# Products of constants on TensorE in the waits around the trunk norms of a two-layer diffusion backbone

## The reference

```python
def rms_norm(x, g):
    xf = x.astype(jnp.float32)
    y = xf * lax.rsqrt(jnp.mean(xf * xf, axis=-1, keepdims=True) + EPS)
    return (y * g.astype(jnp.float32)).astype(x.dtype)

def ffn_sublayer(t, shift, scale, gate, g_pre, g_post, w_in, w_out):
    y = swiglu(modulate(rms_norm(t, g_pre), shift, scale), w_in, w_out)
    return t + FFN_RES * gate * rms_norm(y, g_post)
```

## Time and profile before

| | us |
|---|---|
| median of three runs (lowest, highest) | 3044.97 (3043.56, 3045.20) |
| the profiled execution | 3045.96 |
| its span, first to last instruction | 3044.3 |

### The profile page before, as it was taken

One profiled execution on the slowest core, in us unless ns is written; L12 is line 12 of the kernel. 1 busy time (PEld: TensorE's weight loads), 2 busy tenths in 40 slices (PEclk: granted clock), 3 DMA queues, 4 the chain that ended last, 5 costly groups with the idle time before them and its releaser, 6 DMA issues.

```text
span 3044.3 us, 40240 instructions
## 1 busy us (share of the span) xinstructions
PE 2828.4 (93%) x14410; PEld 2251.5 (74%) x14410; DVE 1623.1 (53%) x2704; ACT 1209.9 (40%) x2223; POOL 220.4 (7%) x291
## 2 busy tenths in 40 slices
PE   6999989997799999997999979999889989999997
PEld 4888857875566676785888848888679667869897
DVE  4677236535544443345566246773365565545764
ACT  3222233235544434434222242222343555555543
POOL 0000011100000000001000010010111000001101
PEclk8999998999899999998999989999989989999899
DMA  5455323320011122132454315553233111324554
GB/s 230 166 193 186 98 96 136 106 90 28 28 42 36 42 77 73 35 118 86 144 172 167 94 54 193 193 191 95 76 108 125 70 56 63 108 84 152 196 174 134
DMA packets 94957, 343.70 MB, mean 113 GB/s; under 512 B 10994, under 2 KB 12786, under 8 KB 92658
## 3 DMA queue, kind: packets, MB, share of 16 engines
q1 hardware_dynamic: 74850, 263.45, 25.5%
q0 software_dynamic: 19984, 78.65, 7.3%
HBM read 337.85 MB, written 4.20 MB: 112 GB/s over the span
## 4 chain that ended last, share of the span: by engine, by line
PE 49%; DVE 4%; issue 4%; ACT 3%; POOL 1%; POOLq 0%; DVEq 0%; ACTq 0%
PE ps L1715 13%; PE ps L1723 13%; PE ps L1716 13%; PE ps L832 2%; PE ps L794 1%; PE ps L811 1%; PE ps L784 1%; DVE work L1526 1%; ACT work L1217 1%; PE ps L1773 1%; PE ps L1770 1%; PE ps L1775 1%; PE ps L790 1%; DVE mx L683 1%; POOL acc L934 1%
## 5 line engine op out<-in xcount | busy, mean ns | idle before, releaser
L1325 DVE TENSOR_TENSOR wlo<-raw,whi 128x1024 fp32r<-128x1024 f32 x492 | 597.4, 1223 | 658.5 <-ACT whi L1071 658.4
L1715 PE MATMUL ps<-xhi,whi 128*128 128x512 f32 (+1 forms) x2304 | 822.7, 368 | 53.7 <-DVE xlo L1559 44.7
L1716 PE MATMUL ps<-xlo,whi 128*128 128x512 f32 (+1 forms) x2304 | 810.3, 363 | 0.0
L1071 ACT ACTIVATE whi<-raw 128x1024 fp32r<-128x1024 f32 x492 | 520.6, 1058 | 565.2 <-PE ps L1723 494.6
L1715 PEld LDWEIGHTS ps<-xhi,whi 128*128 128x128 f32 x2304 | 443.3, 192 | 145.0 <-issue 45.9
L1723 PE MATMUL ps<-xhi,wlo 128*128 128x512 f32 (+1 forms) x2304 | 506.9, 363 | 0.0
L1716 PEld LDWEIGHTS ps<-xlo,whi 128*128 128x128 f32 x2304 | 445.1, 193 | 61.7
L1723 PEld LDWEIGHTS ps<-xhi,wlo 128*128 128x128 f32 x2304 | 396.0, 192 | 63.7 <-issue 0.7
L1473 DVE SCALAR_TENSOR_TENSOR work<-ada,work 128x1024 f32<-128x1024 f32 x256 | 299.3, 1220 | 0.3 <-DMA ada<-in_ada_rows 0.3
L1715 PE MATMUL ps<-ghi,whi 128*128 128x512 f32 (+1 forms) x704 | 252.2, 367 | 1.9 <-ACT whi L1071 1.9
L1716 PE MATMUL ps<-glo,whi 128*128 128x512 f32 (+1 forms) x704 | 251.8, 367 | 0.0
(11 more groups left out here) (199 smaller groups left out, 3373.8 us busy)
## 6 DMA issues: line engine op xcount, KB each, us to landing
raw<-in_ffn_in SPq DMA_DIRECT2D x176, 512.0 KB, 4.7
ada<-in_ada_rows POOLq DMA_DIRECT2D x128, 512.0 KB, 3.8
raw<-in_merge SPq DMA_DIRECT2D x96, 512.0 KB, 3.5
raw<-in_ffn_out SPq DMA_DIRECT2D x64, 512.0 KB, 3.5
raw<-in_qk_a SPq DMA_DIRECT2D x32, 512.0 KB, 3.5
raw<-in_ffn_out SPq DMA_DIRECT2D x32, 384.0 KB, 3.0
raw<-in_qk_b SPq DMA_DIRECT2D x20, 512.0 KB, 3.5
raw<-in_v_a SPq DMA_DIRECT2D x16, 512.0 KB, 3.5
```

What stands on the lines that cost most here:

```text
L1071: act.activation(whi[:, g.ring(SPLIT), :], raw[:, g.ring(RAW), :], ACT.Copy).then_inc(hi_ready, 1)
L1325: dve.tensor_tensor(wlo[:, g.ring(SPLIT), :], raw[:, g.ring(RAW), :], whi[:, g.ring(SPLIT), :].bitcast(F32), ALU.subtract).then_inc(lo_rea ...
L1715: pe.matmul(o, w, hi[:, first + c, 0:tk], start=start, stop=False)
L1716: pe.matmul(o, w, lo[:, first + c, 0:tk], start=False, stop=False)
```

## The change

A helper `keep_busy(n)` issues n products of `ident` (moving, 128 x 128, float32) with `ones` as weights into a bank of PSUM that nobody reads at that time. It carries no wait and signals nothing. For a norm with both halves, `width` is 2 for 512 tokens and 1 for 256, and the calls are:

- 5 x width ahead of the wait for `acc`,
- 12 x width behind the sum of `acc`,
- 2 x width behind each of the first seven sums of squares,
- 17 x width behind the eighth,
- in the first tile of the first product phase behind the norm, 5 products (2 for 256 tokens) for each chunk but the first: behind the wait for that chunk's `xlo` and ahead of its pair of products.

That is 96 products in each of the norms A to D, 48 in E, 35 in the first tiles behind A, B and C and 14 in those behind D and E: 565 in all. So that the first tile can be told from the others, the first iteration of the phase behind each norm is written out (`peel_first`), on all engines.

```diff
+    for before, ph in zip(plan, plan[1:]):
+        if before.kind == "norm" and before.pre and before.post:
+            ph.peel_first = ph.cold = True
...
+            def keep_busy(count):
+
+                for n in range(count):
+                    pe.matmul(ps[:, SCORE, 0:P], ones[:, :], ident[:, :], start=True, stop=True)
+
...
                     o = ps[:, n.ring(BANKS), 0:tk]
+                    if ph.cold and tile == 0 and isinstance(i, int) and i == 0 and c:
+                        keep_busy(5 * tk // T)
                     w = whi[:, s, col:col + P]
...
+                        width = ph.tokens // S
+                        if ph.pre:
+                            keep_busy(5 * width)
                         pe.wait_ge(done["acc"], base(ph, "acc"))
                         stat(ph, 0)
+                        if ph.pre:
+                            keep_busy(12 * width)
...
+                            if ph.post and c < KC - 1:
+                                keep_busy(2 * width)
+                    if ph.post and ph.pre:
+                        keep_busy(17 * width)
```

More of the change, by code:

```diff
@@ L97, in __init__ @@
         self.scale, self.side, self.after = scale, side, after
-        self.peel_first = self.peel_last = False
+        self.peel_first = self.peel_last = self.cold = False
 def ticks_of(ph):
```

## The result

| | us |
|---|---|
| kernel before, median of 6 runs (lowest, highest) | 3045.09 (3042.86, 3045.50) |
| changed kernel, median of 6 runs (lowest, highest) | 3058.03 (3057.12, 3059.15) |
| ratio, changed to before | 1.0044, 95% interval 1.0032 to 1.0057 |

A forecast was written before the change was run, and what follows sets the result against it. The prediction took PE's cold clock to matter only in short stretches behind waits at the norms, with little to give back. Its terms, 0.2 + 12.0 + 2.8 + 0.5 - 1.1 - 1.1 = +13.3 us, gave 3058.3 us, range 3050 to 3070.

The forecast's parts named there:

- ahead of the sum of `acc`: Before each norm's sum of `acc`: 2.2 us of products against a 2.03 us wait, 0.2 us late in all.
- squares, E: Norm E's sums of squares: 6.9 us against 6.35, so 0.5 us lost.
- first tiles behind A, B, C: First tile after these norms: blocks come after the `xlo` wait, a chunk takes 1.57 us, 2.8 us lost in all.
- first tiles behind D, E: First tile of 256 tokens after these norms: each ends 1.1 us earlier.
- The main term: Sums of squares, A to D: blocks make PE the slowest, 3.0 us late per norm, 12.0 for four.
- The wait for the next groups' `whi`: Behind the first tile: a wait there was named as a sign that the prediction was wrong.
- The clock: Norms and first tiles: taken as full from before each norm to past its first tile.
- rival 3: Clock falls in what is left of a wait, squares start at half clock: +11 us, 3069 us; chance 0.09.
- Rival 4: Products of constants don't count, clock falls in the norms as before: 3200 us and more; chance 0.04.
- The price of a product: All blocks: one product of constants costs 0.222 us at full clock, 0.444 at half clock.
- Rival 2: Clock worth more than the blocks cost, in first tiles and E's squares: -9.5 us, 3035.5 us; chance 0.03.
- Written-out iterations: First iterations of the phases behind the norms: no work moves between engines, taken as 0 us.

The follow-up runs named there:

- first experiment: The changed kernel without the products of constants behind the sums of squares; measured 3046.59 us, ratio to before 1.0008.
- the experiment with four products: The changed kernel with four products, not five, behind the first tile's wait for `xlo`, and none behind the sums of squares; measured 3044.14 us, ratio to before 0.9996.

## Why the prediction was right

| term | forecast, us | measured in the profile, us |
|---|---|---|
| ahead of the sum of `acc` | +0.2 | +0.16 (0.04 in each of A to D; in A 433.38 - 429.75 against 433.65 - 430.06) |
| squares, A to D | +12.0 | +11.3 |
| squares, E | +0.5 | +0.48 |
| first tiles behind A, B, C | +2.8 | +3.5 |
| first tiles behind D, E | -2.2 | -1.7 |
| other | 0 | -0.9 |
| sum | +13.3 | +12.8 (+12.7 without the first line, which lies ahead of the stretches) |

The mechanism was right in every term that was given a size. That the number agrees to 0.3 us (3058.3 forecast, 3058.03 measured) is in part luck: the squares came out 0.7 us lower, the tiles behind A to C 0.7 higher, those behind D and E gave back 0.5 less, and "other" took off 0.9, of which 0.5 is the way to the first pair and 0.3 the way from the sum of `acc` to the squares. These errors nearly cancel. They are also smaller than the spread of one kernel's runs, 2 us.

**The main term.** That the four products do not fit between two sums was read from two facts: the last two sums had waited for ACT and DVE in spite of half clock, and PE's new work per chunk, 1.78 us by the rows, is more than the pace of `x`. Both held, though the pace was misread: the forecast took 1.3 us, the eighth part of the 10.56, and it is 1.42 (first experiment), so 0.56 us a chunk was free and not 0.4. The main sum doesn't use it. The four counts in the squares show cause and size: 0, 0.46, 2.83 and 9.09 us per norm for 0, 2, 4 and 8 products. It was set a little high because a sum of 512 columns takes 0.86 us, not four times the 0.22 of 128.

**The first tile.** That a block behind a wait is paid and doesn't fill the wait was right, and the experiment with four products shows it at a size that fits under the pace. The term was sized 0.7 too low for A to C: a chunk takes 1.58 us, not 1.57 (0.07 us in seven), the first block behind the wait takes 0.11 longer, and the second tile 5.48 in place of 5.44. D and E gave 0.25 us less back each. From the start of the block ahead of the seventh pair to tile two's `wlo` products it took 4.35 us in both (2236.69 to 2241.04 behind D), not 4.24, and that block started 0.14 us later behind the first pair than the seventh pair had before. That fits a first pair that comes 0.13 us earlier ("other" in the table) while `xlo` keeps its pace. The wait for the next groups' `whi`, named as a sign of being wrong, did not come in the changed kernel: tile two behind E took 2.87 us. It came only where the first tile was faster still, with the blocks ahead of the wait.

**The clock.** It stayed full in all five norms of the changed kernel, through what is left of the waits (1.01 us in A to D, 1.45 in E): the busy table gives 1.00 for B, C and D too. The price of rival 3 was of the right size: with the 24 products out, a fallen clock cost 10.5 us against the 11 named. Rival 4 falls: with the products of `ident` the clock was 1.00 in all five norms. The Trainium skill's rule that transposes don't hold the full clock ("TensorE: Matmul & The Clock Gate", section "Part 4: PE-mode transpose") does not reach them by that figure, and whether it would reach transposes no run here shows.

**The price of a product.** 0.223 us, as rows 5 gave it. The 81 ns for a 128-column product with its load, which the Trainium skill gives (same page, section "Back-to-back issue gap"), do not hold for a record of this float32 form, which takes 0.111 us: here the measurement decides.

**Rival 2**, that the kernel gets faster, had the right mechanism and the wrong condition. With the blocks ahead of the wait the stretches are 7.9 us shorter than before, near the 9.5 worked out for it; 6.3 of that lie in the first tiles, 0.7 in E's squares and the rest in "other". It doesn't take products that cost nothing: they must stand ahead of the wait and not behind it, with none ahead of the last pair. The forecast named the place as a fault but not as a way.

**Written-out iterations** at 0: shown, within the 1 us that the median can tell.

## What to carry to other kernels

In this kernel half clock cost time only where TensorE was what ended last. So look in each stretch for whether its products wait for another engine in spite of the slow clock, and fill only waits ahead of stretches where they don't. Work put in to hold the clock has a budget, which is the wait less one's own work at full clock, and here it did best ahead of the semaphore's wait and not behind it, and with none ahead of the last piece, whose operand was already there. A higher mean clock is no gain by itself: here it rose from 0.959 to 0.98 and the time rose by 13 us.

## What the runs showed beside that

**Half clock falls differently in a later stage.** The stretch between tile two behind norm A and the sum of `acc` of norm B, which is mostly the attention of layer 0 and which no edit touches, took 912.0 to 918.2 us in the profiles. The busy table of 690 to 1010 us, in turn of the changed kernel, of the one with doubled blocks in the squares, and of the one without the 24 products:

```profile
690.00:1010.00 320.00, 275.75 (x1382) 187.07 (x1380) 164.67 (x435) 161.18 (x422) 11.52 (x9) 0.91 0.11 34
```
```profile
690.00:1010.00 320.00, 275.81 (x1362) 186.94 (x1361) 160.60 (x424) 158.83 (x418) 11.53 (x9) 0.90 0.12 35
```
```profile
690.00:1010.00 320.00, 275.55 (x1395) 186.97 (x1395) 165.46 (x437) 162.25 (x427) 11.54 (x9) 0.92 0.11 34
```

| kernel | untouched stretch, us | clock, 690 to 1010 |
|---|---|---|
| without the 24 products | 912.0 | 0.92 |
| changed | 913.9 | 0.91 |
| no blocks in the tile | 914.3 | 0.91 |
| before; written out only; four products behind the wait | 914.5 | 0.91 |
| only behind the last sum | 916.0 | 0.90 |
| blocks ahead of the wait; halved in the squares | 916.1 | 0.90 |
| no blocks in the squares | 916.6 | 0.90 |
| doubled in the squares | 918.2 | 0.90 |

The lower the clock there, the longer the stretch, in all eleven profiles. That is a part of why the medians of some kernels lie 1 to 4 us off what their stretches give: with the blocks ahead of the wait the median gives 3.4 us less than the stretches, and this stretch is 1.6 us longer than before. The runs of that kernel, which lie near 3035 and near 3041 us with few between, go with the clock too: of eleven, those at 3034.7 to 3037.1 had a mean clock of 0.981 or 0.982, the others 0.980. Only one run of each kernel has a profile, so where in the fast ones the time was saved isn't shown. What decides where the clock falls there, whether it is when the stage begins or something else, was not tried and stays open. For an edit worth a few microseconds the stretches it touches are the better measure.

**PE's waits and the clock.** Waits of 0.63 us between pairs of full-width float32 sums left the clock full (squares without blocks), and waits of 0.76 us between single pairs of `xhi` and `xlo` products let it fall. So the length of a wait alone doesn't tell whether the clock falls. What PE did between the waits differed too, and no run takes the two apart.
